# Loading the weights of experts 5 to 12 as whole 2 MB matrices, with a new order of the hidden features

## The chip, the cores and the metric

The kernel runs on one core of one Trainium2 chip. The metric is the device time of one execution in microseconds (us). A profiled execution records every instruction and every DMA packet of that core. Engines are called as in the profile: PE is the matrix engine (PEld its weight loads), DVE the vector engine, ACT the scalar engine, POOL the GpSimd engine, SP the sync engine, which here issues the DMAs.

## The reference

A trunk of two layers over 256 tokens of 1024 float32 features. Each layer is a mixer (retention and chunked attention in layer 0, sliding-window attention in layer 1), a mixture of 16 experts and a small gated embedding term. The expert part is what matters here:

```python
gates = g_onehot[:, :, None] * (g_w[:, None] * e_gate)[:, None, :]    # top-1 of 4 groups, top-2 of its 4 experts
for gi in range(MOE_GROUPS):
    hg = jnp.einsum('td,edf->tef', t, w_gate[gi])
    hu = jnp.einsum('td,edf->tef', t, w_up[gi])
    act = jax.nn.silu(hg) * hu * gates[:, gi, :, None].astype(t.dtype)
    out = out + jnp.einsum('tef,efd->td', act, w_down[gi])
```

Each expert has three float32 matrices: gate and up of 1024 x 512, down of 512 x 1024. Each is 2 MB, so an expert is 6 MB, a layer's experts 96 MB, and both layers' 192 MB. All of them are read from HBM, whatever the tokens chose.

## The kernel before

The code is written by hand, one instruction stream per engine, with semaphores between them.

**Slots.** SBUF holds nine weight slots of 16 KB per partition (`W`, `NSLOT` = 9), each for one whole matrix, called a unit. `place_units` gives the units of a layer to the slots in turn (the down matrix of expert 2 has places outside the slots), so that a unit takes the slot of the unit nine places before it, which from expert 8 on is the same matrix of the expert three before.

**Loads.** SP issues all expert loads in one queue. Every matrix comes in two halves of 1 MB with 8 KB per partition (`load_half`, L446). For gate and up, partition p holds rows 8p to 8p+7, and a half is four of them. For down, half j is rows 256j to 256j+255, two per partition. From expert 5 on the order is gate half 0, up half 0, gate half 1, up half 1 of expert e (expert 5: both gate halves, then both up halves), and then the two halves of down of expert e-1. Before each half SP waits in `half_reusable` until PE has finished with that half of the slot's old content: `gate_up_halves` or `y_halves` for the first half, `gate_up_ready` or `y_ready` for the second. The queue is served in order of issue.

**PE.** `step(e)` runs gate and up of expert e (`gate_up`, L989), turns the hidden rows of expert e-1 (L998), adds the outputs of expert e-2 into the token sums (L1027), and runs down of expert e-1 (`down`, L1006). For expert 15 the turning and adding stand between the halves. In `gate_up` the 64 rows of the expert are the stationary operand (64 columns), and the weights are the moving one. Each of 8 row groups k takes two matmuls of 512 columns, 256 of gate and 256 of up, which go to the two halves of a bank's partitions. Matmul j takes features 256j to 256j+255, which are unbroken in the slot. A float32 matmul is two instructions in the trace, so gate and up are 32 of them and down 16. PE waits for the first half of both slots ahead of k = 0 (`wait_unit`), and for the second halves ahead of k = 4 (`wait_second`). `down` waits likewise ahead of f = 0 and f = 2.

**Around it.** After a layer's expert 15, PE needs the gate weights of the embedding term and the next layer's projections, which SP loads behind the expert loads in the same queue.

Of the kernel before, what the change touches and what calls it, by code (L numbers as in the profile page):

```python
# [14 lines left out]
P = 128  # L15
D = 1024
KD = D // P
# [34 lines left out]
MOE_SLOTS = (2, 3, 4, 5, 6, 7, 8, 0, 1)  # L52
BETWEEN_SLOTS, END_SLOTS = (4, 5, 6, 7, 8, 0, 1), (4, 5, 6)
OUTSIDE = (U_MOE0 + 8, U_MOE1 + 8)


def expert_units(u0):

    return [u0, u0 + 1] + [u0 + n for e in range(1, NE) for n in (3 * e, 3 * e + 1, 3 * e - 1)] + [u0 + 3 * NE - 1]


def place_units():

    slot, before, landed, second = {}, {}, {}, {}
    last, firsts, seconds = {}, [0] * NSLOT, [0] * NSLOT

    def place(n, s):
        slot[n], before[n] = s, last.get(s)
        last[s] = n
        firsts[s] += 32 if n in (U_OUT1, U_OUT1 + 1) else 16  # L70
        landed[n] = firsts[s]
        if any(u0 <= n < u0 + 3 * NE for u0 in (U_MOE0, U_MOE1)):
            seconds[s] += 16
            second[n] = seconds[s]

    for n in range(6):
        place(n, n)
    for n in range(2):
        place(U_OUT0 + n, n)
    for u0, after, slots in ((U_MOE0, U_GATE0, BETWEEN_SLOTS), (U_MOE1, U_GATE1, END_SLOTS)):  # L80
        for q, n in enumerate(n for n in expert_units(u0) if n not in OUTSIDE):
            place(n, MOE_SLOTS[q % NSLOT])
        for n, s in enumerate(slots):
            place(after + n, s)
    return slot, before, landed, second
# [111 lines left out]
def build(nc, x, p, norm_mix, norm_ffn, norm_ple, final_norm, even_w_in, even_ret_gn, even_rel_bias, even_w_out,  # L197
# [6 lines left out]
    with ExitStack() as ctx:  # L204
# [194 lines left out]
        def _(sp):  # L399
# [29 lines left out]
            def load(srcs, e, m, dst, done):  # L429

                s = srcs[m][e]
                if m < 2:
                    sp.dma_start(dst, s.rearrange("(p k) f -> p (k f)", p=P)).then_inc(done, 16)
                else:
                    sp.dma_start(dst.rearrange("p (j n) -> p j n", j=2), s.rearrange("(j p c) d -> p j (c d)", j=2, c=2))\
                        .then_inc(done, 16)

            def experts(l, u0):
                srcs = (wg_d, wu_d, wd_d)
                def load_half(e, m, n, half, done):  # L440
                    dst, s = unit(n)[:, half * 2048:(half + 1) * 2048], srcs[m][l * NE + e]
                    if m < 2:
                        src = s.rearrange("(p k) f -> p (k f)", p=P)[:, half * 2048:(half + 1) * 2048]
                    else:
                        src = s[256 * half:256 * half + 256, :].rearrange("(p c) d -> p (c d)", c=2)
                    sp.dma_start(dst, src).then_inc(done, 16)  # L446

                def half_reusable(n, half):
# [11 lines left out]

                def outside(f):

                    s = srcs[2][l * NE + 2][256 * (f // 2):256 * (f // 2) + 256, :].rearrange("(p c) d -> p c d", c=2)
                    sp.dma_start(H[:, f - 2, :], s[:, f - 2, :]).then_inc(sem("down2_rest_landed"), 16)

                def load_down(e):

                    n = u0 + 3 * e + 2
                    for half in range(2):
                        half_reusable(n, half)  # L470
                        load_half(e, 2, n, half, (landed, second_landed)[half](n)[0])
# [7 lines left out]
                for e in range(NE):  # L479
                    if e == 3:  # L480
                        load_part(3, 0, 0)
                        load_part(3, 0, 1)
                        sp.wait_ge(sem("side_copied"), 4 * l + 2)
                        sp.dma_start(side_product[l, :, 0, :], XB[:, 0:D]).then_inc(sem("side_first_stored"), 16)
                        sp.wait_ge(sem("side_copied"), 4 * l + 4)
                        for half in range(2):
                            sp.dma_start(side_product[l, :, 1, 512 * half:512 * half + 512], SIDE[1][half])\
                                .then_inc(sem("side_second_stored"), 16)
                        sp.wait_ge(sem("side_second_stored"), 32 * (l + 1))
                        sp.dma_start(XD[:, :], srcs[2][l * NE + 2][0:256, :].rearrange("(p c) d -> p (c d)", c=2))\  # L490
                            .then_inc(sem("down2_landed"), 16)
                        sp.wait_ge(sem("seeded"), 4 * l + 2)
                        outside(2)
                        for half in range(2):
                            load_part(3, 1, half)
                            load_part(4, 0, half)
                            if half == 0:
                                sp.wait_ge(sem("seeded"), 4 * l + 4)
                                outside(3)
                            load_part(4, 1, half)  # L500
                            load_part(3, 2, half)
                    elif e == 5:
                        load_part(5, 0, 0)
                        load_part(5, 0, 1)
                        load_part(5, 1, 0)
                        load_part(5, 1, 1)
                        load_down(4)
                    elif e != 4:
                        for half in range(2):
                            for m in range(2):  # L510
                                load_part(e, m, half)
                        if e == 1 + l:
                            sp.wait_ge(*((sem("ret_out"), 2), (sem("pv1_ready"), 8))[l])
                            for k in range(2):
                                sp.dma_start(WPL[k], ple_w_proj[l, k * P:(k + 1) * P, :]).then_inc(sem("side_weights_landed"), 16)
                        if e >= 1:
                            load_down(e - 1)
# [130 lines left out]
        def _(pe):  # L648
# [224 lines left out]
            def experts(l, u0):  # L873
# [108 lines left out]
                def gate_up(bank, rows, slots, second, halves, parts=(0, 1)):  # L982

                    for k in range(4 * parts[0], 4 * parts[-1] + 4):
                        if k == KD // 2:
                            second()
                        for j in range(2):
                            a = k * FF + j * (FF // 2)
                            mm = pe.matmul(bank[j * BLK:(j + 1) * BLK, :].rearrange("p (m f) -> p m f", m=2), rows[:, k, :],  # L989
                                           W[:, slots, a:a + FF // 2], start=(k == 0), stop=(k == KD - 1))  # L990
                        if k == KD // 2 - 1 and halves is not None:
                            mm.then_inc(halves, 1)
                    return mm
# [49 lines left out]

                def wait_second(*ns):
                    for n in ns:
                        s, w = second_landed(n)
                        pe.wait_ge(s, w)

                def second_half(e, n):
                    if e == NE - 1:  # L1050
# [1254 lines left out]
```

## Time and profile before

| | us |
|---|---|
| median of 3 runs | 732.85 (732.45 to 733.45) |
| span of the profiled execution | 731.3 |
| PE busy in it | 712.4 (97%) |
| DVE busy | 278.0 (38%) |
| ACT busy | 149.7 (20%) |

The span is what the sums go by. It lies 1.5 us below the median of the runs, whose times hold a little that the span does not. A view's times are counted from the span's start. PE's busy time is the union of its instructions, with modelled ends. In the page's slices a digit is a tenth of the slice's time, a slice is 18.3 us, and the DMA line is the mean of 16 DMA engines.

### The profile page before, as it was taken

What the parts mean: (1) busy time and instruction counts of PE and PEld (TensorE: products, weight loads), DVE (VectorE), ACT (ScalarE), POOL (GpSimd) and SP (SyncE); (2) the same over time, 40 slices, a digit from 0 to 9 for tenths busy, and PEclk for the clock granted to TensorE, in tenths of its full rate; (3) what the DMA queues carried; (4) which work ended last, traced back from release to release, by engine and by line L of the source; (5) the groups of instructions that cost most, each with busy time, mean ns of one, the idle gap of its engine ahead of it and who ended that gap; (6) DMA issues with size and microseconds to landing.
All of it is one profiled execution on the core that took longest, in us unless ns stands there. A gap on an engine that the chain in (4) does not pass through costs nothing.

```text
span 731.3 us, 8406 instructions
## 1 busy us (share of the span) xinstructions
PE 712.4 (97%) x3182; PEld 330.4 (45%) x3182; DVE 278.0 (38%) x683; ACT 149.7 (20%) x365; POOL 26.4 (4%) x47
## 2 busy tenths in 40 slices
PE   9999999999999999999999999999999999998996
PEld 6487455564333333333445544464333333332344
DVE  1213361544427242423222563372435424242224
ACT  3000241431111011100321243252111111110132
POOL 0500000000000000000000000000000000000000
PEclk9999999999999999999999999999999999999999
DMA  9998448869999999999999980469999999999941
GB/s 343 363 287 306 171 173 342 333 250 417 422 421 419 420 422 421 421 421 421 395 326 234 419 358 13 173 234 382 416 422 422 419 421 422 420 420 421 407 166 58
DMA packets 50698, 250.89 MB, mean 343 GB/s; under 512 B 4745, under 2 KB 5993, under 8 KB 26081
## 3 DMA queue, kind: packets, MB, share of 16 engines
q1 hardware_dynamic: 48288, 245.04, 85.1%
q0 software_dynamic: 2048, 5.07, 2.3%
q8 instruction: 27, 0.44, 0.2%
q10 hardware_dynamic: 320, 0.22, 0.1%
q14 instruction: 15, 0.11, 0.0%
HBM read 247.15 MB, written 4.73 MB: 344 GB/s over the span
## 4 chain that ended last, share of the span: by engine, by line
PE 86%; DMA 7%; issue 2%; DVE 2%; SPq 1%; ACT 1%; POOLq 0%; POOL 0%; ACTq 0%; DVEq 0%
PE bank L989 26%; PE bank L674 24%; PE bank L1006 13%; DMA weights<-in_moe_w_down_dram 7%; PE bank L1027 4%; PE bank L707 4%; PE bank L949 2%; PE bank L901 2%; PE bank L659 2%; PE bank L998 1%; SPq L446 1%; PE bank L687 1%; PE bank L813 1%; PE bank L1260 1%; PE bank L745 0%
## 5 line engine op out<-in xcount | busy, mean ns | idle before, releaser
L989 PE MATMUL bank<-weights,expert_rows 128*64 128x512 f32 x1024 | 227.2, 593 | 6.8 <-DMA weights<-in_moe_w_up_dram 6.7
L674 PE MATMUL bank<-weights,normalised 128*128 128x512 f32 (+1 forms) x448 | 191.5, 580 | 1.0 <-DVE normalised L1643 0.7
L989 PEld LDWEIGHTS bank<-weights,expert_rows 128*64 128x64 f32 x1024 | 74.5, 137 | 150.1 <-issue 149.9
L674 PEld LDWEIGHTS bank<-weights,normalised 128*128 128x128 f32 x448 | 83.1, 190 | 91.5 <-issue 88.3
L1006 PE MATMUL bank<-weights,hidden_turned_odd 128*64 128x512 f32 x256 | 58.8, 598 | 0.6 <-DMA weights<-in_moe_w_down_dram 0.6
L1006 PE MATMUL bank<-weights,hidden_turned 128*64 128x512 f32 x224 | 51.5, 598 | 1.3 <-DVE hidden_turned L1963 0.6
L1483 ACT ACTIVATE gate_tanh<-bank 128x256 f32<-128x256 f32 x32 | 12.3, 385 | 190.6 <-PE bank L989 190.6
L1345 ACT ACTIVATE expert_outputs<-bank 128x512 fp32r<-128x512 f32 x32 | 19.1, 598 | 123.3 <-PE bank L1006 123.3
L1993 DVE TENSOR_TENSOR gather_onehots<-bank,expert_outputs 128x512 fp32r<-128x512 f32 x32 | 22.1, 692 | 55.5 <-ACT expert_outputs L1345 55.4
L1963 DVE COPY hidden_turned<-bank 128x256 f32<-128x256 f32 x16 | 6.8, 424 | 79.0 <-PE bank L998 79.0
L1963 DVE COPY hidden_turned_odd<-bank 128x256 f32<-128x256 f32 x16 | 6.8, 425 | 77.8 <-PE bank L998 77.8
L1006 PEld LDWEIGHTS bank<-weights,hidden_turned_odd 128*64 128x64 f32 x256 | 16.9, 136 | 34.9 <-issue 31.7
L1975 DVE SCALAR_TENSOR_TENSOR spread_gates<-token_slots,router_temps,token_gates 128x512 f32<-128x512 f32 x32 | 24.0, 751 | 19.6 <-ACT token_gates L1475 18.6
L1006 PEld LDWEIGHTS bank<-weights,hidden_turned 128*64 128x64 f32 x224 | 15.2, 136 | 29.2 <-issue 29.0
L1027 PE MATMUL bank<-expert_outputs,scatter_onehots 64*128 64x512 f32 x128 | 28.4, 441 | 0.0
L707 PE MATMUL bank<-normalised,weights 128*128 128x256 f32 x128 | 28.4, 380 | 0.0
L707 PEld LDWEIGHTS bank<-normalised,weights 128*128 128x128 f32 x128 | 24.1, 190 | 3.7 <-issue 0.5
L1027 PE MATMUL bank<-gather_onehots,scatter_onehots 64*128 64x512 f32 x128 | 25.5, 396 | 0.1
L1345 ACT ACTIVATE expert_rows<-normalised 128x512 f32 (+1 forms) x36 | 20.8, 587 | 11.1 <-issue 7.1
L1978 DVE TENSOR_REDUCE slot_gates<-spread_gates 128x1 f32<-128x512 f32 x32 | 22.0, 686 | 1.1
L998 PEld LDWEIGHTS bank<-constants,hidden 128*128 128x128 f32 x64 | 10.1, 207 | 26.3 <-issue 24.7
L1341 ACT ACTIVATE normalised<-bank,norm_weights 128x128 f32<-128x128 f32 x48 | 13.7, 368 | 33.6 <-PE bank L659 33.3
(267 smaller groups left out, 596.8 us busy)
## 6 DMA issues: line engine op xcount, KB each, us to landing
weights<-in_moe_w_gate_dram SPq DMA_DIRECT2D x64, 1024.0 KB, 16.0
weights<-in_moe_w_up_dram SPq DMA_DIRECT2D x64, 1024.0 KB, 17.3
weights<-in_moe_w_down_dram SPq DMA_DIRECT2D x60, 1024.0 KB, 19.5
weights<-in_even_w_in_dram SPq DMA_DIRECT2D x5, 2048.0 KB, 21.9
weights<-in_ple_w_gate_dram SPq DMA_DIRECT2D x4, 2048.0 KB, 31.7
weights<-in_even_w_out_dram SPq DMA_DIRECT2D x2, 2048.0 KB, 31.5
weights<-in_odd_w_qkv_dram SPq DMA_DIRECT2D x2, 2048.0 KB, 21.2
weights<-in_odd_w_out_dram SPq DMA_DIRECT2D x4, 1024.0 KB, 21.5
```

Of the source, the lines that this page charges most:

```text
L659: mm = pe.transpose(B[banks[half]][:, tok(kk)], H[:, t, 4 * half + kk:D:KD], ident)
L674: mm = pe.matmul(B[bank][:, 0:width], XT[:, k, tok(t)], w[:, k, :], start=(k == 0), stop=(k == KD - 1))
L707: mm = pe.matmul(B[2 * (u % 2) + pair][:, c * SEQ:(c + 1) * SEQ], w[:, k, tok(2 * pair + c)], XT[:, k, :], start=(k == 0), stop=(k == KD - 1))
L901: mm = pe.matmul(B[4 + 2 * t + half][:, :], PINT[:, k, tok(t)], WPL[k][:, half * 512:(half + 1) * 512], start=(k == 0), stop=(k == 1))
L989: mm = pe.matmul(bank[j * BLK:(j + 1) * BLK, :].rearrange("p (m f) -> p m f", m=2), rows[:, k, :], W[:, slots, a:a + FF // 2], start=(k == ...
L998: mm = pe.transpose(B[6][:, c * P:(c + 1) * P], US[:, c:2 * P:2], ident)
L1006: mm = pe.matmul(bank[half * BLK:(half + 1) * BLK, :], hid[:, 2 * (f % 2) + f // 2, :], rows(f)[:, half * 512:(half + 1) * 512], start=(f ...
L1027: mm = pe.matmul(B[sum_bank(t, half)][:, :], PT2[r, par, tok(t)], (YS, PHT)[part][r, par, :], start=False, stop=stop and part == 1)
L1345: return act.activation(dst, src, ACT.Copy)
L1975: stepped(dve.scalar_tensor_tensor(out=SPREAD, in0=SROW.rearrange("p c s -> p (c s)"), scalar=col, in1=WROW.rearrange("p c s -> p (c s)"), ...
L1978: stepped(dve.tensor_reduce(GATES[:, par:par + 1], SPREAD, AX.X, ALU.add), gates)
L1993: dve.tensor_tensor(PHT[:, par, :], bank[:, :], YS[:, par, :].bitcast(F32), ALU.subtract).then_inc(done, 1)
```

## The change

Experts 5 to 12 of each layer (`WHOLE`) are loaded matrix by matrix: one DMA of 2 MB with 16 KB unbroken per partition. The new `load_whole` waits for the second half's semaphore alone, so the slot is given back whole. PE has no second wait for these units. The other experts keep their halves.

All down matrices now lie with rows 4p to 4p+3 in partition p, so that a whole one is unbroken. The hidden features must then be split in the same way: partition q needs features 4q to 4q+3. So `gate_up` of every expert takes features 4q+2j and 4q+2j+1 in matmul j, which is two neighbouring float32 of every four in the slot. Its output is unbroken as before.

```diff
+WHOLE = (5, 13)
...
+def in_one(n):
+
+    return any(u0 + 3 * WHOLE[0] <= n < u0 + 3 * WHOLE[1] for u0 in (U_MOE0, U_MOE1))
...
-        if any(u0 <= n < u0 + 3 * NE for u0 in (U_MOE0, U_MOE1)):
+        if any(u0 <= n < u0 + 3 * NE for u0 in (U_MOE0, U_MOE1)) and not in_one(n):
             seconds[s] += 16
             second[n] = seconds[s]
...
-                        src = s[256 * half:256 * half + 256, :].rearrange("(p c) d -> p (c d)", c=2)
+                        src = s.rearrange("(p f) d -> p (f d)", p=P)[:, half * 2048:(half + 1) * 2048]
...
-                    s = srcs[2][l * NE + 2][256 * (f // 2):256 * (f // 2) + 256, :].rearrange("(p c) d -> p c d", c=2)
-                    sp.dma_start(H[:, f - 2, :], s[:, f - 2, :]).then_inc(sem("down2_rest_landed"), 16)
+                    s = srcs[2][l * NE + 2].rearrange("(p f) d -> p f d", p=P)
+                    sp.dma_start(H[:, f - 2, :], s[:, f, :]).then_inc(sem("down2_rest_landed"), 16)
+
+                def load_whole(e, m):
+
+                    n = u0 + 3 * e + m
+                    half_reusable(n, 1)
+                    load(srcs, l * NE + e, m, unit(n), landed(n)[0])
 
                 def load_down(e):
 
                     n = u0 + 3 * e + 2
+                    if in_one(n):
+                        load_whole(e, 2)
+                        return
...
-                    elif e == 5:
-                        load_part(5, 0, 0)
-                        load_part(5, 0, 1)
-                        load_part(5, 1, 0)
-                        load_part(5, 1, 1)
-                        load_down(4)
+                    elif WHOLE[0] <= e < WHOLE[1]:
+                        load_whole(e, 0)
+                        load_whole(e, 1)
+                        load_down(e - 1)
...
-                            a = k * FF + j * (FF // 2)
-                            mm = pe.matmul(bank[j * BLK:(j + 1) * BLK, :].rearrange("p (m f) -> p m f", m=2), rows[:, k, :],
-                                           W[:, slots, a:a + FF // 2], start=(k == 0), stop=(k == KD - 1))
+                            w = W[:, slots, k * FF:(k + 1) * FF].rearrange("p m (q f) -> p m q f", f=KF)[:, :, :, 2 * j:2 * j + 2]
+                            mm = pe.matmul(bank[j * BLK:(j + 1) * BLK, :].rearrange("p (m q c) -> p m q c", m=2, c=2), rows[:, k, :],
+                                           w, start=(k == 0), stop=(k == KD - 1))
...
-                        s, w = second_landed(n)
-                        pe.wait_ge(s, w)
+                        if n in SECOND:
+                            s, w = second_landed(n)
+                            pe.wait_ge(s, w)
```

SP's queue in layer 0 where the loads of expert 5 begin. Before, the loads of expert 5 and down of expert 4, and then those of expert 6 and down of expert 5 (in brackets the semaphores that a load waits for):

```order
L446 DMA weights<-in_moe_w_gate_dram 128x2048 [waits y_halves]
L446 DMA weights<-in_moe_w_gate_dram 128x2048 [waits y_ready]
L446 DMA weights<-in_moe_w_up_dram 128x2048 [waits gate_up_halves]
L446 DMA weights<-in_moe_w_up_dram 128x2048 [waits gate_up_ready]
L446 DMA weights<-in_moe_w_down_dram 128x2048 [waits gate_up_halves]
L446 DMA weights<-in_moe_w_down_dram 128x2048 [waits gate_up_ready]
L446 DMA weights<-in_moe_w_gate_dram 128x2048 [waits y_halves]
L446 DMA weights<-in_moe_w_up_dram 128x2048 [waits gate_up_halves]
L446 DMA weights<-in_moe_w_gate_dram 128x2048 [waits y_ready]
L446 DMA weights<-in_moe_w_up_dram 128x2048 [waits gate_up_ready]
L446 DMA weights<-in_moe_w_down_dram 128x2048 [waits gate_up_halves]
L446 DMA weights<-in_moe_w_down_dram 128x2048 [waits gate_up_ready]
```

The same place of the changed kernel:

```order
L439 DMA weights<-in_moe_w_gate_dram 128x4096 [waits y_ready]
L439 DMA weights<-in_moe_w_up_dram 128x4096 [waits gate_up_ready]
L451 DMA weights<-in_moe_w_down_dram 128x2048 [waits gate_up_halves]
L451 DMA weights<-in_moe_w_down_dram 128x2048 [waits gate_up_ready]
L439 DMA weights<-in_moe_w_gate_dram 128x4096 [waits y_ready]
L439 DMA weights<-in_moe_w_up_dram 128x4096 [waits gate_up_ready]
L441 DMA weights<-in_moe_w_down_dram 128x4096 [waits gate_up_ready]
```

Two loads of 8 KB per partition became one of 16 KB, which waits for what the later of the two waited for; down of expert 4 stays in halves.

PE in layer 0 where down of expert 10 ends and gate and up of expert 11 (slots 6 and 7) begin. Before:

```order
L1006 MATMUL bank7<-weights,hidden_turned_odd 64x512 [waits ys_low_ready,actt_ready,slot5_landed]
L1006 MATMUL bank7<-weights,hidden_turned_odd 64x512 x3
L1006 MATMUL bank7<-weights,hidden_turned_odd 64x512 [waits slot5_second_landed]
L1006 MATMUL bank7<-weights,hidden_turned_odd 64x512 x3
L989 MATMUL bank5<-weights,expert_rows 64x512 [waits slot6_landed,slot7_landed,act_ready,xe_ready]
L989 MATMUL bank5<-weights,expert_rows 64x512 x7
L989 MATMUL bank5<-weights,expert_rows 64x512 [waits slot7_second_landed,slot6_second_landed]
L989 MATMUL bank5<-weights,expert_rows 64x512 x7
```

And now:

```order
L1018 MATMUL bank7<-weights,hidden_turned_odd 64x512 [waits ys_low_ready,actt_ready,slot5_landed]
L1018 MATMUL bank7<-weights,hidden_turned_odd 64x512 x7
L1001 MATMUL bank5<-weights,expert_rows 64x512 [waits slot6_landed,slot7_landed,act_ready,xe_ready]
L1001 MATMUL bank5<-weights,expert_rows 64x512 x15
L1010 MATMUL bank6<-constants,hidden 128x128 [waits actt_ready,act_ready]
```

The matmuls and their order are the same; the wait in the middle is gone, and the first wait is for the whole matrix.

## Rows read from the trace of the kernel before

**Rows 1.** The page: the span, DMA share and rate in 40 slices, packets.
```profile
span 731.3 us, 8406 instructions
...
DMA  9998448869999999999999980469999999999941
GB/s 343 363 287 306 171 173 342 333 250 417 422 421 419 420 422 421 421 421 421 395 326 234 419 358 13 173 234 382 416 422 422 419 421 422 420 420 421 407 166 58
DMA packets 50698, 250.89 MB, mean 343 GB/s; under 512 B 4745, under 2 KB 5993, under 8 KB 26081
```

**Rows 2.** Windows table: us, PE, PEld, DVE, ACT, POOL busy, PEclk, DMA share, GB/s.
```profile
200.00:345.00 145.00, 141.85 (x684) 51.47 (x682) 52.13 (x118) 17.78 (x33) 0.00 (x0) 1.00 1.01 421
352.50:356.50 4.00, 3.53 (x23) 1.58 (x19) 1.50 (x3) 1.48 (x3) 0.15 (x1) 1.00 1.05 387
```

**Rows 3.** Chain that ended last: start us, us, what; both expert stages.
```profile
261.18 6.87 PE bank L989 x32
...
273.21 6.87 PE bank L989 x32
...
324.77 26.91 DMA weights<-in_moe_w_down_dram
351.72 1.96 PE bank L1006 x8
...
634.92 6.87 PE bank L989 x32
...
663.34 26.67 DMA weights<-in_moe_w_down_dram
```

**Rows 4.** PE timeline of layer 0's last experts: start, us, what, idle before.
```profile
321.75 3.65 PE L989 MATMUL bank<-weights,expert_rows 128*64 128x512 f32 x16 [0.46 <-DMA weights<-in_moe_w_up_dram]
326.70 3.65 PE L989 MATMUL bank<-weights,expert_rows 128*64 128x512 f32 x16 [1.30 <-DMA weights<-in_moe_w_up_dram]
...
336.88 3.65 PE L989 MATMUL bank<-weights,expert_rows 128*64 128x512 f32 x16 [1.38 <-DMA weights<-in_moe_w_up_dram]
```

**Rows 5.** The page's costliest group: line, operation, shapes, count, busy us, idle before.
```profile
L989 PE MATMUL bank<-weights,expert_rows 128*64 128x512 f32 x1024 | 227.2, 593 | 6.8 <-DMA weights<-in_moe_w_up_dram 6.7
```

**Rows 6.** SP timeline where expert 5's slots come free: start, us, loads.
```profile
175.37 2.04 SPq L446 DMA_DIRECT2D weights<-in_moe_w_gate_dram  x2
180.51 3.76 SPq L446 DMA_DIRECT2D weights<-in_moe_w_up_dram  x2
```

**Rows 7.** Line L446, the one issue at 177.1 us: its time to landing.
```profile
L446 SPq DMA_DIRECT2D weights<-in_moe_w_gate_dram x1: 327/327/327, 177.1 to 177.1; - x1
...
DMA to landing us min/median/max: 9.9/9.9/9.9
```

**Rows 8.** Line L446, the issue at 114.0 us, onto an empty queue.
```profile
L446 SPq DMA_DIRECT2D weights<-in_moe_w_down_dram x1: 328/328/328, 114.0 to 114.0; - x1
...
DMA to landing us min/median/max: 4.8/4.8/4.8
```

**Rows 9.** Line L446, the issue at 82.6 us, onto an empty queue.
```profile
L446 SPq DMA_DIRECT2D weights<-in_moe_w_gate_dram x1: 328/328/328, 82.6 to 82.6; - x1
...
DMA to landing us min/median/max: 6.4/6.4/6.4
```

**Rows 10.** Line L446, the issue at 608.1 us: up of expert 12, second half.
```profile
L446 SPq DMA_DIRECT2D weights<-in_moe_w_up_dram x1: 2137/2137/2137, 608.1 to 608.1; - x1
...
DMA to landing us min/median/max: 27.3/27.3/27.3
```

**Rows 11.** Groups of PEld, weight loads of 128 columns: busy us, mean ns, idle.
```profile
L949 PEld LDWEIGHTS bank<-gather_onehots,rows_split 128*128 128x128 f32 x64 | 16.1, 328 | 1.2 <-DVE gather_onehots L1917 0.5 <-issue 0.5
...
L1027 PEld LDWEIGHTS bank<-gather_onehots,scatter_onehots 64*128 64x128 f32 x128 | 12.0, 185 | 2.4 <-DVE gather_onehots L1993 0.9
...
L998 PEld LDWEIGHTS bank<-constants,hidden 128*128 128x128 f32 x64 | 10.1, 207 | 26.3 <-issue 24.7 <-DVE hidden L1988 1.6
```

More of the change, by code:

```diff
@@ L434, in load @@
                 else:
-                    sp.dma_start(dst.rearrange("p (j n) -> p j n", j=2), s.rearrange("(j p c) d -> p j (c d)", j=2, c=2))\
-                        .then_inc(done, 16)
+                    sp.dma_start(dst, s.rearrange("(p f) d -> p (f d)", p=P)).then_inc(done, 16)
             def experts(l, u0):
@@ L489, in experts @@
                         sp.wait_ge(sem("side_second_stored"), 32 * (l + 1))
-                        sp.dma_start(XD[:, :], srcs[2][l * NE + 2][0:256, :].rearrange("(p c) d -> p (c d)", c=2))\
+                        sp.dma_start(XD[:, :], srcs[2][l * NE + 2].rearrange("(p f) d -> p (f d)", p=P)[:, 0:2 * D])\
                             .then_inc(sem("down2_landed"), 16)
```

## The prediction, made before the changed kernel was run

> **What bounds the kernel now.** I read the page's slices first [rows 1]. The DMA engines are full (a 9 in each slice, 417 to 422 GB/s) in two long stretches, slices 10 to 19 and 29 to 38 of 40, which are the two expert stages from the fourth expert or so on. The windows table says the same of 200 to 345 us: DMA share 1.01 and 421 GB/s, while PE is busy for 141.85 of 145 us [rows 2]. Both look full, so the next question is which of them is waited for. The chain of waits has PE in it with a steady period, one expert every 273.21 - 261.18 = 12.03 us [rows 3]. An expert's 6 MiB at 421 GB/s take 6.29 MB / 421 = 14.9 us. So PE is the faster of the two: it starts each stage with experts in stock and eats them up. The reader should see the moment when the stock is gone. It is 321.75 us in layer 0, where PE waits for a load for the first time, and then again: 0.46 + 1.30 + 1.38 = 3.1 us [rows 4]. From there the chain is one DMA step, issued at 324.77 and landed 26.9 us later at 351.7, and the same again for 26.7 us in layer 1 [rows 3]. These 26.9 us are not the latency of one load: on an empty queue 1 MB lands after 4.8 us [rows 8]. They are the queue ahead of it, some 11 MB. Therefore the end of a layer's expert stage is the end of an unbroken DMA stream, and what the stream gains ends the stage earlier, until PE becomes the bound. In both layers together PE idles 6.8 us ahead of gate and up, 6.7 of them on loads [rows 5]. So at most about 3.3 us a layer can be won by any faster stream, and PE has no more than these 3.3 us to lose. The two resources are that close.
>
> **Part 1: longer packets.** The change turns 24 units a layer (8 experts of 3) from 2 DMAs with 8 KB per partition into one with 16 KB. Does the rate depend on the length? At 352.5 to 356.5 us the engines are full with rows of 2 KB (gate weights of the embedding term) and move 387 GB/s, where 8 KB rows move 421 [rows 2]. Per engine, a 2 KB packet takes 16 x 2048 / 387 = 84.7 ns and an 8 KB packet 16 x 8192 / 421 = 311.3 ns. The line through both has (311.3 - 84.7) / 6 = 37.8 ns per KB and 84.7 - 75.5 = 9.2 ns per packet. A packet of 16 KB would take 613.6 ns in place of 622.6. Each engine moves 8 partitions of a unit, so it saves 8 x 9.1 = 73 ns a unit, and a layer 24 x 73 = 1.75 us. One of two completion writes goes too, which I don't count. All of it lies in the full stretch: the loads of experts 5 to 12 begin at 177 us and the queue is never empty until 351.7. It stays below the 3.1 us of PE's waits, so it should arrive whole. Bounds: nothing, if a packet of 16 KB does not exist or costs as its bytes do, and 3.3 us a layer if the stream gains more than the line says. I take 1.75, because the line rests on packets of this queue and this direction. That 8 KB runs do go as one packet is seen in the counts: 50698 - 26081 = 24617 packets are of 8 KB or more [rows 1], and by the code 2 x (96 - 2) = 188 halves go to the slots, and with 2 first halves of the down matrices of expert 2 and 2 loads of the stored side product that is 192 x 128 = 24576 partition rows of 8 KB.
>
> The Trainium skill, "DMA: Bandwidth & Descriptors", section "SWDGE vs HWDGE vs iDMA", speaks against this: a packet is preferably at most 4096 B. By that rule a run of 16 KB would be cut as one of 8 KB is, and part 1 would be 0, which is rival B. The count of packets above doesn't agree for 8 KB.
>
> **Part 2: slots given back whole.** The first half of each unit is no longer issued early. This costs only if the queue runs dry meanwhile. The place to look is the beginning, where the queue is shortest. Gate of expert 5 had its halves issued at 175.37 and 177.08, up at 180.51 and 183.94 [rows 6]. Now they go whole at 177.08 and 183.94. The second half issued at 177.08 landed 9.9 us later, at 187.0 [rows 7], and whole gate lands then too. So up of expert 5 is issued 187.0 - 183.94 = 3.06 us ahead of the end of what is queued. Onto an empty queue 1 MB takes 4.8 to 6.4 us to land [rows 8, 9], of which 2.49 are its bytes; the start-up is 2.3 to 3.9 us. With 3.06 us of work left, between 0 and 0.85 us of stream is lost. I take 0.3, nearer to the usual start-up of 2.3. From expert 7 on the loads of expert e wait for expert e - 3 at PE, whose period is 2.9 us shorter than the stream's, so the lead grows by 2.9 us an expert and the loss is 0 there. Layer 1 has the same order and the same periods: again 0.3.
>
> **Part 3: PE waits for whole matrices.** Landings of second halves stay where they were or come earlier; only a first half that PE needed before its second had landed can cost. The stock is smallest at the last whole expert. Its up matrix landed in layer 1 at 608.1 + 27.3 = 635.4, and PE begins gate and up at 634.92 [rows 3, 10]: late by 0.5 us, less the 22 whole units ahead of it (22 x 73 ns = 1.6 us), plus the 0.3 lost. It is there in time by 0.8 us. If it were not, PE would lose what its later waits of 3.1 us hide anyway. Cost 0, up to 0.5 us.
>
> **Part 4: moving operand of gate and up in pairs.** Every gate and up matmul now reads two neighbouring floats, then skips two. PE's 32 instructions take 6.87 us an expert [rows 3]. No matmul of the trace streams an operand with a gap, so the cost is bounded by the nearest rows, the weight loads [rows 11]. L1027 loads 128 unbroken columns in 185 ns, L998 every second element in 207 ns, L949 every eighth in 328 ns. From below nothing is to be gained: the columns are the same. From above the factor is 328/185 = 1.77; between them L998's 207/185 = 1.12. I take 0, since 6.87 us for 32 instructions that run two side by side are 429 ns for 512 columns, at a granted clock of 1.00 (2.4 GHz) [rows 2] two cycles a column, so that a fetch has slack. The Trainium skill, "SBUF — State Buffer", section "Door 1: The DMA port swizzle", says that SBUF is read in lines of 16 bytes and that two hits a line are enough for full bandwidth. The new pattern has just two, so by the page this part costs nothing; L998 also has two hits and is slower than L1027, so the row leaves a doubt.
>
> **Sum.** Per layer -1.75 + 0.3 = -1.45 us, for two layers -2.9. On the profiled execution 731.3 - 2.9 = 728.4 us; the median of the runs lies 1.5 above the span, so **729.9 us**.
>
> **Rivals.**
> A (forecast). The stream gains 1.75 a layer less small losses: 729.9. Its own range is 728.0 (a net gain of 2.4 a layer, still inside PE's 3.3) to 731.4 (a net gain of 0.7).
> B. No gain: 16 KB runs are cut or cost as bytes do. Then 0.3 to 0.85 a layer is lost: 733.5 (732.9 to 734.5). For it speaks that no 16 KB load of this queue is in the trace; against it, that 8 KB packets are whole.
> C. Slower: PE's reads. Decides at once, since PE's stock of time is 3.1 us over 16 experts: 0.2 us a gate-and-up, 3% of 6.87. At L998's factor it is 0.82 us x 16 = 13.2 a layer, less 3.3: 9.9, so 732.9 + 19.8 = 752.7. At 1.77 it is 5.3 x 16 - 3.3 = 81 a layer, about 895.
> D. The queue runs dry where slots come back whole: 1.6 us at expert 5 and as much again at expert 7, whose gate now goes out at the end of gate and up 4 instead of its middle (3.4 us later). Then 2 x (3.2 - 1.75) = +2.9: 735.8. Against it, the leads of 3 us and more.
>
> **Chances.** A 0.57, B 0.18, C 0.14, D 0.06, and 0.05 for A with so much of D that 731.4 to 734.3 comes out. A measurement of this kernel can tell about 0.2% (1.5 us) from no change. Faster by more: A, 0.57. Within: 0.05 and nearly all of B, 0.22. Slower: C, D and the rest of B, 0.21. The range takes in A, B and part of D, and leaves out C and a little at each end: 728.0 to 735.0.
>
> **What would show it.** Part 1: DMA issues of 2 MB, 16 for gate, up and down each, a DMA rate of 424 to 427 GB/s where it was 421, landings of whole units 4.9 us apart. Part 2: time to landing of up of expert 5 about 8 us; more means that the queue ran dry. Part 3: no idle time of gate and up ahead of expert 13. Part 4: 6.87 us per 32 instructions in the chain; if this row is 7.1 or more, C holds. PE's waits of 3.1 us at the stage's end should shrink to about 1.7 in layer 0. The prediction is wrong if the packets stay at 8 KB, or if PE's period is no longer 12.03.

## The result and the profile after

The changed kernel takes 734.97 us (median of 12 runs, 733.74 to 736.02) where the kernel before, timed beside it, takes 733.04 (12 runs, 731.57 to 735.09). The ratio is 1.0023, with a 95% interval of 1.0015 to 1.0032: slower by about a quarter of a per cent, where 0.4% faster was forecast (729.9).

The page of the changed kernel, to be held against [rows 1]: span, rate in 40 slices, packets. The last line is its costliest group, which answers to [rows 5].

```profile
span 732.9 us, 8342 instructions
...
GB/s 341 368 298 297 163 172 351 323 257 408 401 420 428 428 428 427 421 421 421 393 316 227 416 347 27 173 231 357 402 431 424 427 427 428 424 422 421 405 161 58
DMA packets 43785, 250.88 MB, mean 342 GB/s; under 512 B 3976, under 2 KB 5224, under 8 KB 25312
...
L1001 PE MATMUL bank<-weights,expert_rows 128*64 128x512 f32 x1024 | 237.0, 612 | 0.4 <-DMA weights<-in_moe_w_up_dram 0.4
```

Two things moved, in opposite directions. Where the whole matrices land, the rate is 424 to 428 GB/s a slice and no longer 419 to 422. And the gate and up matmuls of both layers are busy for 237.0 us where they were for 227.2, a mean of 612 ns each against 593; their waits for loads, 6.7 us before, are 0.4. The loads got faster, and PE stopped waiting for them because it got slower.

The windows table of after, for the window of [rows 2] and for a stretch in which only whole matrices are in flight (us, PE, PEld, DVE, ACT, POOL busy, PEclk, DMA share, GB/s). In before the second stretch has 421 GB/s:

```profile
200.00:345.00 145.00, 144.62 (x681) 50.52 (x679) 53.07 (x120) 17.78 (x33) 0.00 (x0) 1.00 1.01 424
240.00:272.00 32.00, 32.00 (x154) 11.14 (x150) 9.29 (x19) 3.92 (x8) 0.00 (x0) 1.00 1.01 428
```

PE is busy for 144.62 of 145 us where it was for 141.85, at the same granted clock of 1.00. The chain that ended last, in after, for the place of [rows 3]:

```profile
251.47 7.20 PE bank L1001 x32
...
263.82 7.20 PE bank L1001 x32
...
308.38 29.76 DMA weights<-in_moe_w_up_dram
338.28 3.82 PE bank L1001 x16
```

The 32 instructions of one gate-and-up take 7.20 us where they took 6.87, and the period of an expert is 263.82 - 251.47 = 12.35 us where it was 12.03. The chain still has a DMA step in layer 0, but it decides nearly nothing, as the PE timeline of after shows for the last two experts. Its last bracket is the only wait for a load that the timeline shows in the stage; [rows 4] had three, of 3.1 us together:

```profile
325.38 7.37 PE L1001 MATMUL bank<-weights,expert_rows 128*64 128x512 f32 x32
...
338.28 3.82 PE L1001 MATMUL bank<-weights,expert_rows 128*64 128x512 f32 x16 [0.38 <-DMA weights<-in_moe_w_up_dram]
```

In layer 1 there is none. So the bound of the expert stage went over from the DMA stream to PE.

**Where the 1.6 us of the span come from.** The starts of PE's first gate-and-up matmul of an expert, and of the first matmul behind the stage (the turning of the residual), taken from the PE records of both traces:

| us | expert 0 | expert 13 | expert 14 | expert 15 | behind the stage | stage |
|---|---|---|---|---|---|---|
| before, layer 0 | 153.2 | 309.1 | 321.8 | 336.9 | 356.4 | 203.2 |
| after, layer 0 | 153.0 | 313.0 | 325.4 | 338.3 | 357.8 | 204.8 |
| before, layer 1 | 490.9 | 646.8 | 660.3 | 675.2 | 694.8 | 203.9 |
| after, layer 1 | 492.3 | 652.3 | 664.6 | 677.0 | 696.3 | 204.0 |

Up to expert 13 the kernel before needs 155.9 us and after 160.0 in both layers: 4.1 us more, 13 times 0.32. In the last two steps before loses what it had gained, since its steps 13 and 14 take 12.7 and 15.1 us in layer 0 and 13.5 and 14.9 in layer 1, where a step without waits takes 12.03. Its waits there are 3.7 and 4.4 us. After loses 0.6 us to loads in layer 0 (its step 14 takes 12.9 us where 12.35 are usual) and nothing in layer 1. What is left over is 1.6 us in layer 0 and 0.1 in layer 1, together 1.7 of the span's 1.6.

### The profile page after: what moved, and what is told of

It is laid out like the page before. It is cut to its first block, busy times and chain, and to the rows that moved or that the text cites. A ratio compares the mean times of both kernels' runs of the same rounds, so it can differ in the third digit from the quotient of the medians.

```text
span 732.9 us, 8342 instructions
## 1 busy us (share of the span) xinstructions
PE 721.1 (98%) x3182; PEld 328.5 (45%) x3182; DVE 278.0 (38%) x683; ACT 149.8 (20%) x365; POOL 26.5 (4%) x47
## 2 busy tenths in 40 slices
DMA packets 43785, 250.88 MB, mean 342 GB/s; under 512 B 3976, under 2 KB 5224, under 8 KB 25312
## 4 chain that ended last, share of the span: by engine, by line
PE 88%; DMA 4%; issue 2%; DVE 2%; SPq 2%; ACT 1%; POOLq 0%; POOL 0%; ACTq 0%; DVEq 0%
PE bank L1001 28%; PE bank L686 24%; PE bank L1018 14%; DMA weights<-in_moe_w_up_dram 4%; PE bank L1039 4%; PE bank L719 4%; PE bank L961 2%; PE bank L913 2%; SPq L451 2%; PE bank L1010 2%; PE bank L671 1%; PE bank L699 1%; PE bank L825 1%; PE bank L1273 1%; PE bank L757 0%
## 5 line engine op out<-in xcount | busy, mean ns | idle before, releaser
L1001 PE MATMUL bank<-weights,expert_rows 128*64 128x512 f32 x1024 | 237.0, 612 | 0.4 <-DMA weights<-in_moe_w_up_dram 0.4
L1001 PEld LDWEIGHTS bank<-weights,expert_rows 128*64 128x64 f32 x1024 | 72.6, 135 | 153.6 <-issue 153.3
L1988 DVE SCALAR_TENSOR_TENSOR spread_gates<-token_slots,router_temps,token_gates 128x512 f32<-128x512 f32 x32 | 24.1, 752 | 20.3 <-ACT token_gates L1488 19.3
```

Source lines behind the costliest of these rows:

```text
L1988: stepped(dve.scalar_tensor_tensor(out=SPREAD, in0=SROW.rearrange("p c s -> p (c s)"), scalar=col, in1=WROW.rearrange("p c s -> p (c s)"), ...
```

## The experiments

Two theories stood at first, and the recorded expectations call the second D or Q. **P**: the strided operand makes each gate-and-up 0.33 us longer, PE becomes the bound, and the longer packets' gain is real but waited for by nobody. **D**: the queue runs dry where slots come back whole (rival D of the prediction, whose 735.8 us is near to the measured time). The first four kernels take the change apart.

### The strided operand alone

The changed kernel, with no matrix loaded whole; expert 5's loads go out in halves and in the order of before again. The down rows, four a partition, and the strided matmuls stay.

```diff
-WHOLE = (5, 13)
+WHOLE = (16, 16)
...
```

> The changed kernel with every expert load in halves as before (8 KB per partition, slots given back by halves). What stays of the change: the rows of down four a partition, and the gate and up matmuls that read two neighbouring floats of every four. Theory P (the matmuls cost it): gate and up take 7.20 us an expert, not 6.87, as in the changed kernel; PE uses up the time that it waited for loads, and the kernel takes 735 to 737 us against 733. Rival Q (the slots given back whole cost it, by an empty queue at expert 5, and PE's slower matmuls are hidden behind the DMA stream): no more than 733.5.

Measured: 734.87 us (734.47 to 736.45), ratio 1.0039 (1.0025 to 1.0054), just below P's 735 to 737 and well above Q's 733.5. The costliest group of its page:

```profile
L1007 PE MATMUL bank<-weights,expert_rows 128*64 128x512 f32 x1024 | 237.0, 612 | 0.2 <-DMA weights<-in_moe_w_up_dram 0.2
```

The same 237.0 us and 612 ns as in after, and the waits are gone as well. So the whole loss is there with 8 KB packets and early halves. What this kernel still shares with after beside the strided operand is the new order of the down rows; the kernel "every second column" below hasn't got it, and its group shows the same 612 ns. The interval overlaps that of after, so what the 16 KB loads add or save beside it can't be told here.

### Whole gate and up, with unbroken matmuls

The kernel before, with gate and up of experts 5 to 12 loaded whole; down keeps its halves and its layout, so that the matmuls read unbroken features.

```diff
+WHOLE = (5, 13)
...
+    return any(u0 + 3 * WHOLE[0] <= n < u0 + 3 * WHOLE[1] and (n - u0) % 3 < 2 for u0 in (U_MOE0, U_MOE1))
...
+                    elif WHOLE[0] <= e < WHOLE[1]:
+                        load_whole(e, 0)
+                        load_whole(e, 1)
+                        load_down(e - 1)
```

> The kernel before with gate and up alone of experts 5 to 12 as one DMA of 2 MB and 16 KB per partition, slots given back whole; down stays in halves of two rows a partition, and the gate and up matmuls read unbroken columns. Theory P: 6.87 us for gate and up; 16 packets' worth of units save 16 x 0.08 = 1.3 us a layer, and the queue runs dry at expert 5 for 1.3 us in layer 0 and 0.8 in layer 1 (as in the changed kernel), so 732 to 733.5. Rival Q: the same loss without the longer packets of down, slower than before, 734 or more.

Measured: 733.94 us (732.66 to 735.82), ratio 1.0023 (1.0012 to 1.0033), above what P expected and just under the 734 of its rival. PE is as fast as before and waits as before:

```profile
L999 PE MATMUL bank<-weights,expert_rows 128*64 128x512 f32 x1024 | 227.0, 593 | 6.3 <-DMA weights<-in_moe_w_up_dram 6.3
```

So P alone isn't all there is: with PE out of the way, this kernel should have shown the packets' gain. The issue of expert 5's up matrix in layer 0, and its time to landing, say where it went:

```profile
L439 SPq DMA_DIRECT2D weights<-in_moe_w_up_dram x1: 328/328/328, 184.2 to 184.2; - x1
...
DMA to landing us min/median/max: 10.0/10.0/10.0
```

It landed at 194.15. Gate of expert 5 had landed at 186.85, 7.3 us earlier, where 2 MB take 4.9 us: it is 2.4 us late. The windows table of the place shows DMA engines that idle for a part of the time, where before has a share of 1.01 and 423 GB/s:

```profile
184.00:191.00 7.00, 7.00 (x38) 2.91 (x38) 4.11 (x8) 1.62 (x3) 0.00 (x0) 1.00 0.93 357
```

The missing bytes are 7 x (423 - 357) / 423 = 1.1 us of stream; PE waits for the last packet of a load, and that one was 2.4 late. In layer 1 up of expert 5 came out on time. The stages taken as in the table above are 204.2 and 202.7 us, so +1.0 in layer 0 and -1.2 in layer 1. The second is the gain that the prediction's Part 1 gives for 16 matrices, 16 x 73 ns = 1.2 us; the first is that gain with the 2.4 lost, -1.2 + 2.4 = +1.2.

Late landings aren't all dry queues, though. In layer 1 of this kernel up of expert 6 is 1.1 us late with 5.7 us of work ahead of it, and from 538 to 548 us the DMA share is 1.00 at 421 GB/s. Before has such a place too (the down half issued at 574.9, 1.0 us late behind a queue of 17 us), and after has one (issued at 276.2, 1.4 us, behind 21 us), both with a DMA share of 1.01 around the landing. Their cause is open. Two stages can differ by about a microsecond through them alone.

The profiled execution was at the low end of the runs (span 731.4), so in the median run the loss is probably larger; that part is inferred.

### Late halves

The kernel before with 8 KB packets, but both halves of a matrix of experts 5 to 12 issued when its slot is given back whole. This is D's mechanism without anything else.

```diff
                 def half_reusable(n, half):
...
+                    if u0 + 15 <= n < u0 + 39:
+                        half = 1
...
-                    elif e == 5:
-                        load_part(5, 0, 0)
-                        load_part(5, 0, 1)
-                        load_part(5, 1, 0)
-                        load_part(5, 1, 1)
+                    elif 5 <= e < 13:
+                        for m in range(2):
+                            for half in range(2):
+                                load_part(e, m, half)
```

> The kernel before, all loads in halves of 8 KB per partition, but for experts 5 to 12 both halves wait until the slot is given back whole. Only the return of the slots is changed. Theory P: the queue is empty for about 1.3 us at expert 5 of layer 0 and 0.8 in layer 1, nothing gives it back, and the end of each stage moves by that: 733 + 2 = 735. Rival Q expects the whole loss of the changed kernel here too and nothing from the matmuls: 735. If PE's waits at the stage's end stay 3.1 us, the stream is the bound; the time of gate and up tells P from Q in the other runs.

Measured: 736.19 us (734.49 to 738.56), ratio 1.0051 (1.0032 to 1.0070), above the 735 that was expected. All waits of PE by what it waited for, the first line:

```profile
PE bank L990 <- DMA weights<-in_moe_w_up_dram: 9.8, 8, 1.3
```

The waits for loads rise from 6.7 to 9.8 us, and the stages are 205.5 and 205.4 us, 2.3 and 1.5 longer. The first half of up of expert 5 lands 1.7 us late in layer 0 and 1.2 in layer 1, with a DMA share of 0.97 and 0.95 around it (183 to 191 and 523 to 531 us) where before has 1.02. Layer 0 has one more late landing, 1.5 us at the up half issued at 232.8, behind a queue of 15 us, so it doesn't come from the late halves. So D's mechanism exists and costs more than the prediction's 0.3 a layer, in a kernel whose bound is the stream.

### Whole gate and up from expert 6 on

As the second kernel, with `WHOLE = (6, 14)`: expert 5 keeps its halves.

```diff
+WHOLE = (6, 14)
```

> As gu_whole, but for experts 6 to 13: the loads of expert 5 stay in halves, where the queue is shortest. Theory P: the queue has 4 us or more of work at every whole issue (the shortest lead is at gate of expert 7, 3.9 us), so the 1.3 us a layer of the longer packets arrive almost whole: 730.5 to 731.5. Rival: if the loss at expert 5 only moves to expert 7, 732 to 733.5.

Measured: 730.56 us (729.62 to 731.87), ratio 0.9972 (0.9963 to 0.9981). This beats both kernels. Its windows table, its PE timeline in layer 0 and its costliest group:

```profile
240.00:272.00 32.00, 32.00 (x158) 11.64 (x156) 11.20 (x23) 4.26 (x8) 0.00 (x0) 1.00 1.01 426
```

```profile
310.92 7.09 PE L1005 MATMUL bank<-weights,expert_rows 128*64 128x512 f32 x32 [1.30 <-DMA weights<-in_moe_w_up_dram]
...
335.78 3.65 PE L1005 MATMUL bank<-weights,expert_rows 128*64 128x512 f32 x16 [0.58 <-DMA weights<-in_moe_w_up_dram]
```

```profile
L1005 PE MATMUL bank<-weights,expert_rows 128*64 128x512 f32 x1024 | 226.5, 593 | 4.4 <-DMA weights<-in_moe_w_up_dram 4.4
```

The stages are 201.7 and 202.4 us, 1.5 less in each layer (0.3 more than 16 x 73 ns), and the waits for loads fall from 6.7 to 4.4. One expert's difference in where whole loads begin is worth 3.4 us (733.94 against 730.56). The late landing at expert 5, 2.4 us in the one profiled execution, is the part of it that a trace shows.

### Everything whole from expert 6 on

The changed kernel with `WHOLE = (6, 14)`. If the dry queue at expert 5 made after slow, this one would be as fast as the one above.

```diff
-WHOLE = (5, 13)
+WHOLE = (6, 14)
...
```

> The changed kernel with experts 6 to 13 instead of 5 to 12 as whole transfers; expert 5 stays in halves, so that the queue does not run dry there. The strided matmuls stay. Theory P (PE's slower matmuls alone set the changed kernel's time, its DMA stream has time to spare): no gain from it, 734 to 735.5, gate and up 7.20 us, PE hardly waits for loads. Rival Q (the dry queue at expert 5 is what makes the changed kernel slow): 732.5 to 733.5.

Measured: 734.17 us (733.39 to 734.84), ratio 1.0013 (1.0004 to 1.0022). Its costliest group:

```profile
L1007 PE MATMUL bank<-weights,expert_rows 128*64 128x512 f32 x1024 | 237.1, 612 | 0.5 <-DMA weights<-in_moe_w_up_dram 0.5
```

The queue doesn't run dry at expert 5 here. In layer 1 two loads land late a little further on, up of expert 6 by 1.3 us and gate of expert 7 by 1.2 (395 GB/s from 547 to 557 us); PE's waits of 0.5 us say that it notices little. In layer 0 nothing there lands late and PE has no wait for a load, yet the stage takes 204.0 us where the unbroken matmuls take 201.7. The time stays 3.6 us above theirs. With the kernel of the strided operand alone, which has no whole load, that settles it between P and D for the changed kernel: the 237.1 us hold it back. The 0.8 us against after are within what the two intervals leave open.

### What the moving operand pays for

These kernels change only which weights of the slots the gate and up matmuls of the kernel before read, so they compute other features than the reference. Each was run once. SBUF is addressed in bytes, and "stretch" is used here for 16 aligned bytes, four floats.

Every second column:

```diff
-                            a = k * FF + j * (FF // 2)
+                            w = W[:, slots, k * FF + j:(k + 1) * FF:2]
```

> The kernel before, but each gate and up matmul reads every second column of its 512 (gate and up) instead of one half of them: single floats with gaps of one float, the same number of 16-byte stretches touched as in the changed kernel. The features come out in another order than down expects, so the output is not the reference's. Theory L (the price goes with how many 16-byte stretches a matmul touches): 7.20 us for the 32 instructions, as in the changed kernel. Rival R (it goes with the length of the unbroken runs): more than 7.20.

```profile
239.45 7.20 PE bank L989 x32
```

735.68 us, with the costliest group at 237.1 us, 612 ns each, as in after. Four floats of every eight:

```diff
+                            w = W[:, slots, k * FF:(k + 1) * FF].rearrange("p m (q f) -> p m q f", f=8)[:, :, :, 4 * j:4 * j + 4]
```

> The kernel before, but each gate and up matmul reads four neighbouring floats of every eight. The features come out in another order than down expects, so the output is not the reference's. Theory L (16-byte stretches touched, here as few as in the kernel before): 6.87 us for the 32 instructions. Rival R (short runs): between 6.87 and 7.20. Rival S (any pattern that is not one unbroken run costs the same): 7.20.

```profile
236.95 6.87 PE bank L989 x32
```

732.78 us. One float of every four:

```diff
+                            w = W[:, slots, (k // 4) * 2048 + (k % 2) * 1024 + j:(k // 4) * 2048 + (k % 2) * 1024 + 1024:4]
```

> The kernel before, but each gate and up matmul reads one float of every four over 1024 columns: twice as many 16-byte stretches as in the changed kernel. It multiplies other weights than the reference, so the output is not the reference's. Theory L: the price over 6.87 us is at least twice as large as in the changed kernel (7.5 us or more); PE is then the bound and the kernel takes 740 us or more. Rival S (any broken pattern costs the same): 7.20.

```profile
250.10 14.39 PE bank L989 x32
```

963.64 us. The expectation set 7.5 us as the least for this row, and it is about twice that. Each row is a full gate-and-up between 236 and 252 us in the chain of waits of that kernel. A gap as such costs nothing (four of eight: 6.87, as unbroken). Two floats used of a stretch cost 7.20, whether they are neighbours, as in the change, or not. One float costs 14.39. An instruction of 512 columns touches 256 stretches in the second case and 512 in the third: 7.20 us / 32 / 256 = 0.879 ns and 14.39 us / 32 / 512 = 0.878 ns. Unbroken, 128 stretches would be 113 ns, less than the 215 ns that 512 columns take anyway. All these prices are a 32nd of the row. The two matmuls of a pair run side by side, so each instruction itself lasts about twice as long. This gave a rule (S) that four more kernels put to the test.

Every third float:

```diff
+                            w = W[:, slots, (k // 4) * 2048 + (k % 2) * 1024 + j:(k // 4) * 2048 + (k % 2) * 1024 + 768 + j:3][:, :, :FF // 2]
```

> Each gate and up matmul reads every third float of a stretch of 768 (step 3 through other weights of the same slot; the features that are computed are therefore not the reference's). A column takes 4/3 as many columns per 16-byte stretch: 384 stretches per 512 columns. Theory S (an instruction takes 512 columns at 215 ns in all, or its 16-byte stretches at 0.88 ns each, whichever is more; from 7.20 us / 32 / 256 = 0.879 ns and 14.39 us / 32 / 512 = 0.878 ns): 32 x 384 x 0.88 ns = 10.8 us per gate-up, and about 733.3 + 32 x 3.93 - 10.3 = 849 us in all (step of one float in four: 32 x 7.52 = 240.6 us more at PE gave 230.4 more in all). Rival J (every column that jumps costs the same, wherever it lands): 14.4 us and about 963 us, as one float in four.

```profile
248.66 10.85 PE bank L989 x32
```

851.36 us. S holds to 0.5% (10.8), and a fixed price for each jump is out.

One float of every eight:

```diff
+                            w = W[:, slots, (k // 4) * 2048 + j:(k // 4) * 2048 + 2048:8]
```

> Each gate and up matmul reads one float of eight (through other weights of the same slot; the features that are computed are not the reference's). Theory S (price per 16-byte stretch touched): 512 stretches per instruction, 14.4 us per gate-up and about 963 us, the same as one float in four. Rival B (price per byte passed over, or lines of 32 bytes): 28.8 us, or about 1420 us in all.

```profile
251.63 14.69 PE bank L989 x32
```

973.31 us. It is not the bytes passed over: 14.69 against 14.39, 2% more, which S doesn't explain.

Four floats across the border of two stretches:

```diff
+                            w = W[:, slots, k * FF:(k + 1) * FF].rearrange("p m (q f) -> p m q f", f=8)[:, :, :, 2 * j + 1:2 * j + 5]
```

> Each gate and up matmul reads four floats of every eight, floats 1 to 4 (first column tile) or 3 to 6 (second), so that each run of four lies across the border of two 16-byte stretches (some features are computed twice and some not at all, so the output is not the reference's). Theory S (stretches touched, 256 per instruction): 7.20 us per gate-up and about 735.5 us, though the run of four with no border in it took 6.87. Rival A (bytes used per run count, not where they lie): 6.87 us and about 733 us.

```profile
248.78 8.54 PE bank L989 x32
```

776.93 us. Where the run lies matters (6.87 with no border in it), but S's 7.20 is wrong too. Its plain form adds up the stretches of an instruction and compares the sum with the columns. If the comparison is made stretch by stretch, each one costs 0.879 ns or 0.42 ns (215 / 512) for each column in it, whichever is more. The three floats are 1.26 ns and the single one 0.88, together 2.14 for four columns, 128 times: 274 ns, 8.76 us for 32. Measured is 8.54, so time saved on one stretch helps the next only a little. The same form gives 7.20, 10.8 and 14.4 for the other three. It was made after the result, so it fits these and was not tested on another pattern; the 2% of one float in eight stay outside it.

The strided read for one column tile of the two that run side by side:

```diff
+                            at = (k // 4) * 2048 + (k % 2) * 1024
+                            w = W[:, slots, at:at + 1024:4] if j == 0 else W[:, slots, at:at + FF // 2]
```

> The first column tile's matmul reads one float in four, the second's reads 256 + 256 unbroken floats (other weights of the slot; the features that are computed are not the reference's). The two run side by side. Theory Q (both draw on one supply of stretches): a pair has 512 + 128 stretches, 640 x 0.88 x 16 = 9.0 us per gate-up, about 733.3 + 32 x 2.13 - 10.3 = 791 us. Rival R (each side goes at its own pace, and the slower one sets the pair's): 14.4 us and about 963 us. Between the two (the slow side alone pays, one after the other): 16 x (450 + 215) ns = 10.6 us, about 842 us.

```profile
250.52 14.50 PE bank L990 x24
```

966.67 us. The 14.50 us of the row are the whole gate and up of an expert, though only 24 of its 32 instructions are in the chain (the others end beside them). That is 14.39 within 1%: the tiles don't share a supply of stretches. Each goes at its own pace, and the slower one sets the pair's (rival R of the expectation).

## Why the prediction was wrong

The forecast was 729.9 us, 2.9 below before, and the changed kernel is 1.9 above. The stated range, 728.0 to 735.0, just holds the 734.97, and that is luck: it was set to take in A, B and part of D and to leave out C, and C is what came.

**What bounds the kernel** was right: two resources 3 to 4 us a layer apart, with the stream ahead. PE's cover was put at 3.3 us a layer; measured by its steps it is 3.7 and 4.4.

**Part 1** was right in size and worth nothing. Packets of 8 KB and more went from 24617 to 43785 - 25312 = 18473. That is 6144 fewer, just the 48 matrices x 128 rows that became one packet each. At 428 GB/s one takes 16 x 16384 / 428 = 612.5 ns, where 613.6 were forecast. The Trainium skill, "DMA: Bandwidth & Descriptors", section "SWDGE vs HWDGE vs iDMA", prefers packets of 4096 B or less. The Trainium skill says so there of the descriptors that GpSimd builds, and the prediction held it against loads of SP. For SP's queue these counts and rates show packets of 16 KB, and at a better rate than those of 8 KB. The error was to take the gain as time. It shortens the stage only as long as PE would otherwise wait, and PE no longer did. Where PE kept its speed, the gain arrived (layer 1 of whole gate and up: -1.2 us; from expert 6 on: -1.5 a layer).

**Part 2** was priced too low. The SP timeline of after, and the landing of the second of these loads:

```profile
177.42 0.33 SPq L439 DMA_DIRECT2D weights<-in_moe_w_gate_dram  x1
184.62 0.33 SPq L439 DMA_DIRECT2D weights<-in_moe_w_up_dram  x1
```

```profile
L439 SPq DMA_DIRECT2D weights<-in_moe_w_up_dram x1: 328/328/328, 184.6 to 184.6; - x1
...
DMA to landing us min/median/max: 9.8/9.8/9.8
```

Gate took 10.8 us and landed at 188.2; up was issued 3.6 us ahead of that and landed at 194.4, 6.2 us behind gate where 4.9 are its bytes. So 1.3 us were lost (0.8 in layer 1), where 0.3 were taken and 0.85 was the bound. Call the work still queued at an issue the lead. The prediction took the loss as a start-up of 2.3 to 3.9 us less the lead. In the traces of after and of the whole and late kernels, eleven loads from expert 5 on were issued with a lead under 4 us. Six landed 0.8 to 2.4 us late, at leads of 2.7 to 3.7, and lead plus loss is 3.8 to 5.1 us there. Five, at leads of 3.0 to 4.0, were on time. So it is no fixed start-up, and what decides is open. In the changed kernel the slow PE covered nearly all of this loss, in the kernels with unbroken matmuls nothing did.

**Part 3** was right for the changed kernel: PE waits for no whole matrix. It owes that to Part 4's failure in part, since a slower PE needs them later. With unbroken matmuls PE waits 0.79 us for expert 12 in layer 0 of whole gate and up, and 1.30 and 1.92 us for expert 13 in the kernel from expert 6 on.

**Part 4 is the step that failed.** It was taken as 0 and measured 0.33 us per gate-and-up, 4.8% of 6.87. The price lay between the bounds given (1.0 and 1.12), and the threshold given, 0.2 us, was passed, so rival C held, with a size between its threshold and its lowest price. With the measured term, C's own sum gives 16 x 0.33 - 3.3 = 2.0 us a layer and a span of 731.3 + 4.0 = 735.3. It came out at 732.9: the cover was 8.1 us (3.7 + 4.4) for both layers up to expert 15 where 6.6 were taken, and the part behind it, which holds one more gate-and-up of 0.33, got no longer (19.5 to 19.5 us, 19.6 to 19.3 by the table), so a little cover was there too. Two inferences misled me. The first: "429 ns for 512 columns, two cycles a column, so a fetch has slack". It has, but nearly all of it is used up with two floats a stretch: 2 x 0.42 = 0.84 ns for the columns against 0.88 for the stretch. The second was the rule of the Trainium skill, "SBUF — State Buffer", section "Door 1: The DMA port swizzle", that two hits on a line of 16 bytes are enough. The size of the line agrees with the runs (one float of a stretch costs 2.1 times, four of eight nothing), but two are not quite enough here: 7.20 against 6.87 us. That section of the Trainium skill also says that each access that crosses to a new line pays a penalty, which the prediction passed over; with two floats used of a line there are twice as many such crossings a column as with four. In a kernel with 3 us of cover on PE for 16 such steps, 4.8% decides. The doubt that I had noted, that the weight loads with two hits took 207 ns against 185, pointed the right way. L1027's loads are of 64 partitions, though; against the unbroken loads of 128 partitions in L674, 190 ns by the page of before, the factor is 1.09, nearer to the 1.05 measured.

**Rival D** came nearest in its number, 735.8, and was not the cause: without the whole loads of expert 5 the changed kernel is at 734.17, and with no whole load at all at 734.87. **Rival B** is out by the packets.

## What to carry to other kernels

When two resources are within 2% of each other, price every edit on both; a change that speeds up the one that is waited for by 2 us and slows the other by 5 is a loss, however small the 5 are as a share. Keep a float32 moving operand on whole aligned runs of four floats, or accept 5% at two and a factor of two at one. A load that gives up an early half for a longer packet should not start where the queue is shortest: whole gate and up from expert 5 on gave 733.94 us, and from expert 6 on 730.56, 0.28% below the kernel before, both with unbroken matmuls. And one trace a kernel is a thin ground for differences of a microsecond: single late landings of that size turn up in the kernel before too.

## What the runs showed of the hardware

The time of a float32 matmul with 512 moving columns (two side by side, granted clock 1.00, which is 2.4 GHz) depends on how the columns lie in stretches of 16 bytes. As a 32nd of a gate-and-up it is 215 ns with four floats of each, 225 with two, 339 with every third float, 450 with one of four, 459 with one of eight, and 267 with runs of four that cross a border. Packets of 16 KB exist in SP's queue and bring the stream from 421 to 428 GB/s. A queue that still holds 3 to 4 us of work can run dry when the next 1 or 2 MB are issued (late in six of eleven such places, by 0.8 to 2.4 us). And a load can land 1.0 to 1.5 us late behind 15 to 21 us of queue, with a DMA share of 1.01.
